# Sample attention in a two-layer decoder step: cached values as the streaming operand instead of the weights

## What is computed

```
def dilated_attn_sample(q, k_new, v_new, cache, window, dil, slopes):
    keys = jnp.concatenate([cache[:, :, 0], k_new], axis=1)
    vals = jnp.concatenate([cache[:, :, 1], v_new], axis=1)
    idx = L + jnp.arange(S)[:, None] - taps[None, :] * dil
    kg, vg = keys[:, idx], vals[:, idx]
    s = jnp.einsum('bshe,bsthe->bhst', q, kg) * HD ** -0.5 - slopes * (taps * dil)
    lse = jax.nn.logsumexp(s, axis=-1)
    p = jnp.exp(s - lse[..., None])
    o = jnp.einsum('bhst,bsthe->bshe', p, vg)
```

## Time and profile before

| what | us |
|---|---|
| median of 3 runs | 2577.85 (2577.38 to 2577.85) |
| the profiled execution | 2579.57 |
| its span, first to last instruction | 2577.4 |
| PE busy in the span | 2460.5 (95%) |
| DVE busy | 1519.7 (59%) |
| ACT busy | 807.5 (31%) |
| mean granted clock of TensorE | 0.96 |

### The profile page before, as it was taken

One profiled execution on the slowest core, in us unless ns is written; L12 is line 12 of the kernel. 1 busy time (PEld: TensorE's weight loads), 2 busy tenths in 40 slices (PEclk: granted clock), 3 DMA queues, 4 the chain that ended last, 5 costly groups with the idle time before them and its releaser, 6 DMA issues.

```text
span 2577.4 us, 47464 instructions
## 1 busy us (share of the span) xinstructions
PE 2460.5 (95%) x19531; PEld 2253.0 (87%) x19531; DVE 1519.7 (59%) x3350; ACT 807.5 (31%) x1066; POOL 162.7 (6%) x122
## 2 busy tenths in 40 slices
PE   8999999999999999999899998999999999999997
PEld 3587877898999999999877878778989999999996
DVE  1121189878855873875346111898788558747753
ACT  2311321333253244233211113213332532443342
POOL 0240500000000000000112005000000000000000
PEclk9999999999999999999998578999999999999998
DMA  4333334343444444434665013343334444444342
GB/s 178 108 123 114 131 117 144 116 143 120 147 162 149 147 147 163 148 133 149 195 185 153 1 50 131 115 140 122 134 127 141 161 156 147 147 163 148 130 150 80
DMA packets 51248, 348.91 MB, mean 135 GB/s; under 512 B 6112, under 2 KB 6128, under 8 KB 11408
## 3 DMA queue, kind: packets, MB, share of 16 engines
q1 hardware_dynamic: 44928, 324.16, 36.9%
q0 software_dynamic: 6192, 22.95, 3.1%
HBM read 342.83 MB, written 4.26 MB: 135 GB/s over the span
## 4 chain that ended last, share of the span: by engine, by line
PE 93%; DVE 3%; ACT 2%; issue 1%; POOL 0%; DMA 0%; DVEq 0%; ACTq 0%; POOLq 0%
PE ps L594 19%; PE ps L600 18%; PE ps L595 18%; PE ps L584 10%; PE ps L568 5%; PE ps L494 3%; PE ps L517 2%; PE ps L772 2%; PE ps L449 2%; PE ps L450 2%; PE ps L451 2%; PE ps L706 1%; ACT C_hi L940 1%; PE ps L693 1%; PE ps L830 1%; PE ps L476 1%
## 5 line engine op out<-in xcount | busy, mean ns | idle before, releaser
L1264 DVE TENSOR_TENSOR w_lo<-ring,w_hi 128x1024 fp32r<-128x1024 f32 x448 | 544.8, 1223 | 269.6 <-ACT w_hi L930 262.8
L930 ACT ACTIVATE w_hi<-ring 128x1024 fp32r<-128x1024 f32 x448 | 473.1, 1057 | 636.2 <-PE ps L595 635.5
L594 PE MATMUL ps<-C_hi,w_hi 128*128 128x288 f32 x2048 | 630.3, 308 | 20.8 <-DVE C_lo L1319 20.4
L600 PE MATMUL ps<-C_hi,w_lo 128*128 128x288 f32 x2048 | 606.7, 296 | 0.0
L595 PE MATMUL ps<-C_lo,w_hi 128*128 128x288 f32 x2048 | 600.7, 293 | 0.0
L594 PE MATMUL ps<-h_hi,w_hi 128*128 128x288 f32 x1536 | 461.3, 300 | 3.9 <-DVE slots L1272 3.9
L595 PE MATMUL ps<-h_lo,w_hi 128*128 128x288 f32 x1536 | 454.6, 296 | 0.0
L600 PE MATMUL ps<-h_hi,w_lo 128*128 128x288 f32 x1536 | 453.3, 295 | 0.0
L594 PEld LDWEIGHTS ps<-C_hi,w_hi 128*128 128x128 f32 x2048 | 386.1, 189 | 26.7 <-DVE C_lo L1319 20.0
L595 PEld LDWEIGHTS ps<-C_lo,w_hi 128*128 128x128 f32 x2048 | 389.7, 190 | 0.0
L600 PEld LDWEIGHTS ps<-C_hi,w_lo 128*128 128x128 f32 x2048 | 386.5, 189 | 0.0
(11 more groups left out here) (211 smaller groups left out, 2553.1 us busy)
## 6 DMA issues: line engine op xcount, KB each, us to landing
ring<-in_U SPq DMA_DIRECT2D x128, 1024.0 KB, 4.9
ring<-in_V SPq DMA_DIRECT2D x128, 1024.0 KB, 4.9
ring<-in_peer_q SPq DMA_DIRECT2D x16, 1024.0 KB, 4.9
ring<-in_w_in_v SPq DMA_DIRECT2D x8, 1024.0 KB, 7.5
ring<-in_w_in_u SPq DMA_DIRECT2D x8, 1024.0 KB, 4.9
ring<-in_w_out SPq DMA_DIRECT2D x8, 1024.0 KB, 4.9
work<-in_cache POOLq DMA_DIRECT2D x8, 512.0 KB, 5.4
big<-in_cache POOLq DMA_DIRECT2D x8, 512.0 KB, 7.1
```

The source lines that it names most:

```text
L594: one = pe.matmul(out, w_hi[:, h % HI_SLOTS, at], hi, start=start, stop=False)
L600: return pe.matmul(out, w_lo[:, h % (2 * R), at], hi, start=False, stop=stop)
L930: act.activation(w_hi[:, k % HI_SLOTS, :], ring[:, bl % R, (k % 2) * HBLK:(k % 2 + 1) * HBLK], ACT.Copy).then_inc(hi_made, 1)
L1264: dve.tensor_tensor(w_lo[:, n % (2 * R), :], ring[:, n // 2 % R, n % 2 * HBLK:(n % 2 + 1) * HBLK], w_hi[:, n % HI_SLOTS, :], ALU.subtract) ...
```

## The change

- The sample products swap operands: a matmul now has 16 columns of probabilities (four heads by four tokens of one sample) as its weights and 256 columns of cached values as its streaming operand. Its 16 result rows lie at partitions 0, 32, 64 or 96, by sample, and four samples in a row write side by side. For groups 1 and 2 each token has its own cached rows; the weights are cut out of a zero-filled buffer `PsM` so that the other tokens' columns are zero. `PsN` holds the weights of the new rows. There are 72 such matmuls and 6 of the new rows, in place of 144 and 6; they are shared out in twelfths over units 0 to 5.
- The results have tokens on partitions, so ACT copies them out (three copies of 512 columns) at the end of unit 5, PE turns them with 12 transposes in unit 6, and ACT copies them into `hT` with 24 small instructions.
- ACT writes the turned probabilities with six instructions where there were three; DVE clears `PsM` and `PsN` with two memsets after `q_lo`.
- The keys of all eight samples get a place of their own in `big`, where later the values go: POOL issues all 24 key loads first, then `skT`, `sbias` and `dist`, then the values of a sample when DVE has used its keys. `Kc` is no longer double buffered.
- The norm for keys and values goes to a buffer of its own, `hkv`, so DVE writes it at once after the norm for the queries.
- Unit scores lie in PSUM bank 4 (even units) or banks 5 and 6 (odd units), and PE waits for one older unit to be read rather than tile by tile; DVE waits for all three tiles of a unit. The units' other tiles use two banks in turn instead of three, which leaves banks 2, 3 and 7 for the sample products.

```diff
@@ -248,10 +248,18 @@
 PpTs = [view(mid, 4608, 6, P), view(work, 768, 6, P)]
-PsT = view(mid, 5376, 6, P)
+PsM0 = view(work, 3840, NB, 4 * NS)
+PsM = view(work, 3968, 2, NB, 64)
+PsN = view(mid, 5376, NG, NB, 32)
+sampled = view(work, 1536, 2 * NG, 256)
 Vc = view(big, 0, NB, KV)
-Kc = view(work, 0, 2, KV)
-prod = view(work, 2 * KV, 16, HD)
+Kc = Vc
+prod = view(work, 0, 16, HD)
+hkv = view(work, 1536, DC, T)
@@ -364,9 +374,6 @@
     pool.wait_ge(x_ready, 2)
-    pool.dma_start(skT[:], i["skT"]).then_inc(sub_keys_loaded, 16)
-    pool.dma_start(sbias[:], i["sbias"]).then_inc(sbias_loaded, 16)
-    pool.dma_start(dist, i["dist"]).then_inc(dist_loaded, 16)
@@ -377,9 +384,12 @@
     for b in range(NB):
-        if b >= 2:
-            pool.wait_ge(k_used, b - 1)
-        load_cache(Kc[:, b % 2, :], b, 0, k_landed[b % 2])
+        load_cache(Kc[:, b, :], b, 0, k_landed[b])
+    pool.dma_start(skT[:], i["skT"]).then_inc(sub_keys_loaded, 16)
+    pool.dma_start(sbias[:], i["sbias"]).then_inc(sbias_loaded, 16)
+    pool.dma_start(dist, i["dist"]).then_inc(dist_loaded, 16)
+    for b in range(NB):
+        pool.wait_ge(k_used, b + 1)
@@ -690,7 +700,7 @@
                 at = (j * DC + c) * P
-                last = pe.matmul(ps[:, b, 0:T], ring[:, r, at:at + P], hT[:, c, :],
+                last = pe.matmul(ps[:, b, 0:T], ring[:, r, at:at + P], hkv[:, c, :],
@@ -729,12 +739,20 @@
         last.then_inc(dve_full, 1)
+    def prompt_place(u, g):
+        n = P * (u % 2 + 1)
+        bank, at = (4, g * P) if u % 2 == 0 else (5 + g // 2, g % 2 * 256)
+        return ps[:, bank, at:at + n]
...
         for g in range(NG):
-            b = dve_bank("ps", 3 * u + g)
-            pe.matmul(ps[:, b, 0:P * (m + 1)], aq[row:row + HD, 2 * g + h // 2, m * P:(m + 1) * P],
+            if g == 0:
+                pe.wait_ge(dve_free, D0["ps"] + 3 * max(u - 1, 0))
+            pe.matmul(prompt_place(u, g), aq[row:row + HD, 2 * g + h // 2, m * P:(m + 1) * P],
@@ -754,42 +772,45 @@
     last.then_inc(act_full, 1)
+    def sample_place(half, g):
+        n = half * NG + g
+        return ps[:, (2, 3, 7)[n // 2], n % 2 * 256:n % 2 * 256 + 256]
     def sample_products():
-        for g in range(NG):
-            for pr in range(2):
-                dst = ps[:, 3, (g * 2 + pr) * 64:(g * 2 + pr + 1) * 64]
-                dst3 = dst.rearrange("p (j t) -> p j t", j=2)
-                yield pe.matmul(dst, av[0:NSAMP, 2, g * 256 + pr * P:g * 256 + (pr + 1) * P],
-                                PsT[0:NSAMP, 3 + g, pr * 64:(pr + 1) * 64], start=True, stop=False,
-                                skip_group_check=True)
-                prob = PsT[0:CK[g], g, pr * 64:(pr + 1) * 64].rearrange("p (j t) -> p j t", j=2)
-                for b_ in range(NB):
-                    for s in range(CS[g]):
-                        w = NS // CS[g]
-                        t0 = NS * b_ + s * w
-                        at = COFF[g] + s * 256 + pr * P
-                        yield pe.matmul(dst3[:, :, t0:t0 + w], Vc[0:CK[g], b_, at:at + P],
-                                        prob[:, :, t0:t0 + w], start=False,
-                                        stop=(b_ == NB - 1 and s == CS[g] - 1), skip_group_check=True)
+        for half in range(2):
+            for g in range(NG):
+                dst = sample_place(half, g)
+                cols = slice(g * 256, (g + 1) * 256)
+                yield pe.matmul(dst, PsN[0:NSAMP, g, 4 * half:4 * half + 4, :].rearrange("p b r -> p (b r)"),
+                                av[0:NSAMP, 2, cols], start=True, stop=False, skip_group_check=True)
+                for s in range(CS[g]):
+                    at = COFF[g] + s * 256
+                    for k in range(4):
+                        b_ = 4 * half + k
+                        prob = PsM0[:, b_, :] if g == 0 else PsM[0:CK[g], g - 1, b_, 15 * s:15 * s + 16]
+                        yield pe.matmul(dst[32 * k:32 * k + 16], prob, Vc[0:CK[g], b_, at:at + 256],
+                                        start=False, stop=(s == CS[g] - 1), skip_group_check=True)
...
     sample = sample_products()
-    nsample = 2 * sum(1 + NB * s for s in CS)
+    nsample = sum(2 + NB * s for s in CS)
...
         last = None
-        for _ in range(share(k, 16, nsample), share(k + 1, 16, nsample)):
+        for _ in range(share(k, 12, nsample), share(k + 1, 12, nsample)):
...
     def unit_bank(kk):
-        if kk >= 3:
-            pe.wait_ge(act_free, A0["pp"] + kk - 2)
-        return kk % 3
+        if kk >= 2:
+            pe.wait_ge(act_free, A0["pp"] + kk - 1)
+        return kk % 2
@@ -797,7 +818,8 @@
             prompt_scores(u + 2)
-        sample_share(2 * u)
+        if u < 6:
+            sample_share(2 * u)
@@ -805,9 +827,18 @@
             last.then_inc(act_full, 1)
-        last = sample_share(2 * u + 1)
-        if u == 7:
+        if u < 6:
+            last = sample_share(2 * u + 1)
+        if u == 5:
             last.then_inc(samples_full, 1)
+        if u == 6:
+            pe.wait_ge(samples_moved, 1)
+            for half in range(2):
+                for g in range(NG):
+                    for pr in range(2):
+                        last = pe.transpose(sample_place(half, g)[:, pr * P:(pr + 1) * P],
+                                            sampled[:, half * NG + g, pr * P:(pr + 1) * P], ident[:])
+            last.then_inc(samples_turned, 1)
@@ -1042,11 +1073,22 @@
     b = full("sp", 0)
-    act.activation(PsT[:, 0:2, :].rearrange("p a b -> p (a b)"), ps[:, b, 0:256], ACT.Copy)
-    act.activation(PsT[0:CK[2], 2, :], ps[0:CK[2], b, 256:384], ACT.Copy).then_inc(act_free, 1)
+    act.wait_ge(masks_cleared, 2)
+    for g in range(NG):
+        n = CK[g]
+        turned = ps[0:n, b, g * P:(g + 1) * P].rearrange("p (h b t) -> p b t h", h=4, b=NB)
+        if g == 0:
+            dst = PsM0.rearrange("p b (h t) -> p b t h", h=4)
+        else:
+            dst = PsM[0:n, g - 1].rearrange("p b (s h t) -> p b s h t", s=NS, h=4)[:, :, :, :, 0]
+        last = act.activation(dst, turned, ACT.Copy)
+    last.then_inc(act_free, 1)
     b = full("sp", 1)
-    act.activation(PsT[0:NSAMP, 3:6, :].rearrange("p a b -> p (a b)"), ps[0:NSAMP, b, 0:384],
-                   ACT.Copy).then_inc(act_free, 1)
+    for g in range(NG):
+        last = act.activation(PsN[0:NSAMP, g, :, 0:16].rearrange("p b (h t) -> p b t h", h=4),
+                              ps[0:NSAMP, b, g * P:(g + 1) * P].rearrange("p (h b t) -> p b t h", h=4, b=NB),
+                              ACT.Copy)
+    last.then_inc(act_free, 1)
@@ -1056,18 +1098,34 @@
             act.activation(PpTs[m][:, 3 * half:3 * half + 3, :].rearrange("p a b -> p (a b)"),
-                           ps[:, kk % 3, 0:384], ACT.Copy).then_inc(act_free, 1)
+                           ps[:, kk % 2, 0:384], ACT.Copy).then_inc(act_free, 1)
...
         for g in range(NG):
-            last = act.activation(dst[:, 2 * g + h // 2, :], ps[row:row + HD, kk % 3, g * P:(g + 1) * P], ACT.Copy)
+            last = act.activation(dst[:, 2 * g + h // 2, :], ps[row:row + HD, kk % 2, g * P:(g + 1) * P], ACT.Copy)
...
         kk += 1
-    act.wait_ge(samples_full, 1)
-    o3 = ps[:, 3, 0:384].rearrange("p (c j t) -> p c j t", c=AC, j=2)
-    act.activation(hT[0:HD, 0:AC, NPROMPT:T], o3[0:HD, :, 0, :], ACT.Copy)
-    act.activation(hT[HD:P, 0:AC, NPROMPT:T], o3[HD:P, :, 1, :], ACT.Copy).then_inc(samples_out, 1)
+        if u == 5:
+            act.wait_ge(samples_full, 1)
+            for k, bank in enumerate((2, 3, 7)):
+                last = act.activation(sampled[:, 2 * k:2 * k + 2, :].rearrange("p a b -> p (a b)"), ps[:, bank, :],
+                                      ACT.Copy)
+            last.then_inc(samples_moved, 1)
+        if u == 6:
+            act.wait_ge(samples_turned, 1)
+            for n in range(2 * NG):
+                half, g = n // NG, n % NG
+                for pr in range(2):
+                    turned = ps[:, (2, 3, 7)[n // 2], n % 2 * 256 + pr * P:n % 2 * 256 + (pr + 1) * P].rearrange(
+                        "p (b r) -> p b r", b=4)
+                    for j in range(2):
+                        rows, at = slice(j * HD, (j + 1) * HD), NS * (2 * pr + j)
+                        last = act.activation(
+                            hT[rows, 2 * g + pr, NPROMPT + 16 * half:NPROMPT + 16 * half + 16].rearrange(
+                                "p (b t) -> p b t", b=4), turned[rows, :, at:at + NS], ACT.Copy)
+            last.then_inc(samples_out, 1)
@@ -1125,12 +1183,12 @@
         dve.tensor_tensor(eh_lo[:, c, :], hT[:, c, :], eh_hi[:, c, :], ALU.subtract).then_inc(eh_lo_made, 1)
-    def scaled(gain, split=None):
+    def scaled(gain, split=None, out=hT):
...
                 early_lower_h(split, c - 2)
-            dve.scalar_tensor_tensor(out=hT[:, c, :], in0=xT[:, c, :], scalar=gains[:, gain, c:c + 1],
+            dve.scalar_tensor_tensor(out=out[:, c, :], in0=xT[:, c, :], scalar=gains[:, gain, c:c + 1],
```

(32 more changed lines are left out.)

## The result

| | before | after |
|---|---|---|
| median of the runs, us | 2577.85 | 2540.12 (2539.31 to 2547.84) |
| ratio to before, 95% interval | | 0.9858 [0.9845, 0.9870] |
| profiled execution, us (its span) | 2579.57 (2577.4) | 2539.31 (2537.2) |

The change is 37.7 us (1.5%) faster. Two executions far from all others (6016 us of the kernel before, 3402 us of the last experiment) are left out of the medians and ranges.

The account below looks back on a forecast made before the run. PE was taken to bind. At full clock units 0 and 1 (16.6), units 2 to 5 (23.6), tail (12.0), 0.6, 0.3 and 1.5 make 54.6 of 106.7 us; with 3.7 ahead, 56 gained: 2522, range 2514 to 2549.

Parts of the forecast that it names:

- a fall of the clock between units: Sign of being wrong, in the units: the granted clock would drop again between units.
- the main case: Whole kernel: four-way overlap and a full clock, 56 us gained, 2522 us; chance 0.54.
- What bounds: Whole kernel: PE, busy 2460.5 of 2577.4 us; only shortening its work or waits, or a faster clock, pays.
- Sample products: Units 0 to 5: 18 fours and 6 wide ones, 22 us at half clock, 11 at full; a twelfth 1.9 or 0.95.
- The expected pitch of 0.057 us: Sign of being right: wide-matmul records in the units 0.057 us apart in the mean at full clock, 0.114 at half.
- Form changes: Units: changing between forms of matmul 24 times, 1.5 us allowed, bounds ±1.5.
- Units at full clock: Units 2 to 5: waits on ACT's copy and DVE's normalising make 5.7 us per even unit, 6.1 per odd one.
- Which clock: Units: clock rises to full in unit 1 or so and doesn't fall afterwards, PE's gaps being short.
- The half-clock rival: Units: clock stays at 0.50, matmuls overlap four at a time; stretch 74 us, 36 gained, 2542; chance 0.3.
- Little overlap, full clock: Units: little overlap, PE's work binds at full clock; stretch 71.6 us, 39 gained, 2539; chance 0.1.
- Tail: From the end of unit 5's copy: 15.6 us at half clock, 12.0 at full, with 2.4 for 24 small copies.
- The rest: Outside the units: norm buffer 1.3 + 1.7 us gained, keys at once 0.7; late values nothing, at worst 10 us.

Follow-up runs that it names:

- the last experiment: The kernel after with filled waits and eight-copy tail, plus filling matmuls behind the sums of norms 2, 3 and 4; 2519.78 us, ratio 0.9765.
- the kernel with fillers: The kernel after, with unused f16 matmuls of 256 columns placed where PE would wait, from the last spread query on; 2519.25 us, ratio 0.9777.
- The kernel with the other order and fillers: The kernel after with filled waits and the sample products' loops swapped, the quarter changing every 8 records for groups 1 and 2; 2531.12 us, ratio 0.9811.
- eight copies: The kernel after, its twelve transposes writing three neighbouring banks so ACT makes 8 copies of 64 x 48 instead of 24 of 64 x 16; 2531.45 us, ratio 0.9815.
- one norm buffer: The kernel after with the norm of keys and values written over `hT` again, behind ACT's query copies; 2541.45 us, ratio 0.9855.
- keys in turn: The kernel after with keys loaded two samples ahead again, each next one when DVE has used one; 2538.62 us, ratio 0.9858.

## Why the prediction was right, and where it wasn't

- **The total** is right in part by luck. It lies in the range because the range reached over two rivals, and neither they nor the main case is what happened: the prediction's own sign of being wrong, "a fall of the clock between units", showed.
- **What bounds** held: PE in the units; 36.3 of the 40.2 us came from there.
- **Sample products.** The overlap is right. In the trace of the kernel with fillers, at full clock, four wide records begin some 7 ns apart and the next four 0.21 us later, so four matmuls cost 0.43 us, where 0.456 was forecast; a twelfth of 14 records takes 1.83 and 0.98 us (half and full clock) for 1.9 and 0.95. A wide matmul of the new rows takes 1.15 and 0.62 us for 0.91 and 0.456, the end of its row included. One thing was sized too small: the rows between other work hold 3, 4, 6 or 7 matmuls and not always fours: 6 records take 0.55 us as 8 take 0.56, so 22 fours are paid for and not 18, some 1.7 us at full clock. The expected pitch of 0.057 us shows within a row only: with the row's end it is 0.070.
- **Form changes.** Allowed 1.5 us. Each row of the wide kind pays some 0.12 to 0.17 us at its end at full clock (0.55 for one group of eight against 0.43 within a row; 0.62 for a new-row pair against 0.456). A twelfth with a new-row matmul in its middle costs 0.55 + 0.62 + 0.55 = 1.72 us. Over 14 rows and six new-row matmuls that is an estimated 2.7 us of PE's time for the 1.5 allowed. It is of the kind that the Trainium skill's TensorEngine Tiling page (Key Properties) calls a drain, and small; the sum came out all the same, 53.7 for 54.6.
- **Units at full clock.** About right, once the clock is held: from unit 2's normalised tile to unit 4's is 1430.16 less 1417.45 in the kernel with fillers, 12.7 us for two units, where 5.7 + 6.1 = 11.8 was forecast. By parts of that kernel: units 0 and 1 took 14.2 us (to DVE's start on unit 2 at 1415.09) for the forecast's 16.6, since with fillers ahead of them the clock was down from 1403.9 to 1407.3 us only; units 2 to 5 took 25.5 (to 1440.64) for 23.6; the tail 13.9 for 12.0, the small copies' 2.2 us more. So 53.7 against 54.6 holds as a sum of errors of both signs of some 2 us each.
- **Which clock.** This step failed: "I expect the rise there, in unit 1 or so, and no fall afterwards, since PE's gaps are short there". The rise came at 1410.3 us, at the start of unit 1, as forecast. But PE's idle time of 1.74 us in units 2 and 4, 3.57 in unit 6 and 4.92 in unit 7 was enough: the clock fell at 1420.5, 1441.0, 1458.0 and 1468.3. The forecast had counted those gaps ("PE idle some 2 us per unit") and called them short without a row for a gap of that size. The stretch became 70.5 us, between 54.6 and 74: units 0 and 1 took 16.5 us, as forecast, units 2 to 5 37.1 for 23.6, the tail 16.9 for 12.0. Against the kernel with fillers the three are 2.3, 11.5 and 2.9 us longer. The 15.9 us over 54.6 are most of the forecast's error of 18 us.
- **The half-clock rival** (2542) was near in time and wrong in kind: 0.70, not 0.50.
- **Little overlap, full clock** (2539) was even nearer in time, and is refuted by the spacing of the records. The kernel with the other order and fillers comes closest to what it describes: 2531.
- **Tail.** 24 small copies were 2.4 us in the sum, with 4.8 as the bound; they took 4.55, 0.19 us from one to the next. The allowance of 0.1 us for the overlap of neighbours was wrong for them. The three wide copies (1.56 us) lay in ACT's wait for DVE, as forecast.
- **The rest.** Norm buffer: 1.3 + 1.7 forecast, 3.4 measured. Keys at once: 0.7 forecast, 0. Late values: nothing, and PE waits for no transfer in the units. What the forecast left out: the output projection found the clock up (23.6 us for the earlier trace rows's 25.76), 2.2 us, and 1.5 us lost further on, for which I have no cause.

That several sums end near 2540 shows why the total couldn't decide between the cases: the granted clock by window, and the fillers, did.

## What to carry to other kernels

If PE's work is cut, look at where it will wait next, and read the granted clock of the windows around those waits: here PE's idle times in the units, 13.3 us in all, and those just ahead of them cost another 16.8 us by the half clock behind them, and matmuls that nobody reads, put into those waits, gave that back. Matmuls with few weight columns were cheap here when neighbours went to different partition quarters one after another, and the loop order decided it. An edit that loses PE time can show no loss while the clock alternates, so measure it again with the clock held.

## What was not expected

- Four matmuls of 16 weight columns and 256 streamed columns, in four quarters, run in 0.43 us within a row where one alone takes 0.456; with the quarter changing every eight records 14 records take 2.27 us for 0.98. In that order only records around the change from one quarter to the next overlap; within a quarter each starts 0.216 us behind the last.
- Taking out all 72 wide products left the stretch at 62.1 us, longer than the 53.7 with them at a held clock.
- PE, at half clock and busy for 13.56 of 13.60 us, was followed by full clock in the change, while the kernel before was busy for 104.48 of 106.8 us and stayed at 0.50. The same share of busy time on the page isn't the same to the clock; what in the narrow matmuls makes the difference is not settled, and one filler behind each hardly changed it (0.54).
- The transposes, of which the prediction feared that they would not hold the clock, brought it up: from 1458.0 to 1461.4 us PE worked on 15 transposes and on nothing else (3.27 of 3.40 us), and the clock went from 0.51 to 0.99 behind them. The traces of three experiments with the same tail (eight copies, one norm buffer, keys in turn) show it too.
- A copy of 64 x 16 from PSUM takes ACT 0.19 us, one of 64 x 48 0.215: at these sizes the number of instructions is what costs.
